# The last retained row's norm in three pieces, the output weights split by two engines, and the first output product one pair later

## The chip, the cores and the metric

One core of a Trainium2 chip runs the whole block. The metric is the device time of one execution in microseconds. TensorE multiplies, VectorE, ScalarE and GpSimd do the elementwise work, SyncE issues most of the transfers, and every engine works off its own queue in order and waits on semaphores for the others.

## What is computed

A streaming-encoder block of one layer on 1024 tokens of 1024 features, in f32. The input is normed and modulated (scale and shift from a conditioning vector), projected, and mixed by two groups of heads; group A is a sparse attention with 8 heads of 64, group B a retention with 8 heads of 64 and a norm of each head:

```python
    y = (inner + cross).reshape(B, S, H, d)
    mu = jnp.mean(y, axis=-1, keepdims=True)
    var = jnp.mean(jnp.square(y - mu), axis=-1, keepdims=True)
    y = (y - mu) * lax.rsqrt(var + EPS)
    return (jax.nn.silu(g.astype(jnp.float32)) * y).astype(dt).reshape(B, S, H * d)
...
    y = jnp.concatenate([y_a, y_b], axis=-1)
    return jnp.einsum('bse,ed->bsd', y, w_o)
```

The result is added to the input with a gate; after a second modulated norm a router sends each token to two of 32 small experts, and a last norm ends the block.

## The kernel before

Tokens lie on the 128 partitions, in 8 tiles (T = 8). Every large product is split: a number is written as a high part, rounded to the array's fast f32 format, and a low part, which is the rest, and `split_product` adds high times high, high times low and low times high, three matmuls of 512 columns for each 128 of depth. For each weight ScalarE therefore copies the high part and another engine subtracts it from the weight to get the low part.

**Start.** TensorE makes the row of modulation (L1770), ScalarE copies it out of PSUM (L833), and TensorE turns it into columns (L1777): groups g = 0, 1 are the two halves of the shift, g = 2, 3 those of the scale, each in PSUM bank g. One signal, `pe_cols`, stands behind all of them. VectorE adds the biases (L1126 to L1128) and then works in four parts of two k (blocks of 128 of depth): `hidden` modulates the normed input (L1134), ScalarE copies high parts (L849, L842), and `split_low` (L1183) and `hidden_low` (L1191) make the low ones. TensorE starts the input projection when the first low parts are there (L1748 to L1750).

**Retention.** For each tile t, `b_finish` on VectorE takes the values from PSUM (`b_yread`), then norms each head: mean, difference (L1409 to L1411), square and its mean (L1412 to L1414), gate (L1416), and a multiplication with the root that GpSimd makes (L712, L1418). SyncE stores the row (`store_retained`, L550). For the last tile the first step runs with the retention and all of the rest behind the first pair of heads of the attention, as one piece.

**Attention.** A list `order`, the same for all engines, sets the order of the work: tile after tile (i = 0 to 7) four pairs of heads (`heads`), then `rows`, with the products of earlier tiles between the pairs (`between`). A pair costs: logits on TensorE (L1898), `negated_logits` on VectorE (L1349), `exponent` on ScalarE (L954), turning of the weights on TensorE (L1974), their copy out of PSUM by ScalarE (L990), and the product with the values (L1987). TensorE issues the logits of the next pair ahead of the turning of this one. VectorE's logits run two heads ahead, so behind pair p it does those of pair p + 1. `rows` turns the sums' reciprocals (L1539, L2024) and the retained row (L2031) and makes high and low parts of the joined rows (L1544 to L1551; ScalarE L1003, L1006). `mix` is the output product of a tile in two halves of 512 columns, 24 matmuls each, with two VectorE operations (L1564, L1566) that scale it with the gate and add the input. `norm` and `turn` make the second norm (ScalarE L1012, GpSimd L725, VectorE L1573 to L1579) and turn it (L1755), `route` is the router's product.

The first `mix` needs the output weights in high and low parts, 8 blocks of 128x1024. They are loaded in two halves, blocks 4 to 7 (L584) and 0 to 3 (L588). ScalarE copies two blocks behind each of the four pairs of tile 0 (L998), in the order 4, 5, 6, 7, 0, 1, 2, 3. GpSimd subtracts for blocks 4 to 7 (L719), VectorE for blocks 0 to 3, behind the last pair of tile 0 and the first of tile 1 (L1532). SyncE's queue then has the store of the last retained row and a wait for it, ahead of all loads of the tiles: the retained row of tile 0 (L597), its input (L604), and four loads for the second norm and the router (L606 to L609). GpSimd waits for the last four and multiplies `sc2` with `g` (L721).

```python
        between[1] = [[], [("mix", (0, 0))], [("mix", (0, 1))], []]
```

## Time and profile before

| | us |
|---|---|
| three runs | 1575.22, 1575.89 (median), 1576.64 |
| profiled execution | 1575.17 |
| its span | 1573.0 |
| TensorE busy in it | 1420.4 (90%) |
| VectorE busy | 1098.9 (70%) |
| ScalarE busy | 906.5 (58%) |
| GpSimd busy | 272.8 (17%) |

The span runs from the first to the last instruction; the execution has some 2 us around it. Busy times say which engine is nearly full over the whole span, but a change in one place is worth what the waits of that place say. The granted clock is a share of TensorE's 2.4 GHz: 1.00 is 2.4 GHz and 0.50 is 1.2 GHz; its mean over the span is 0.955.

### The profile page before, as it was taken

How to read it: one execution, taken by the hardware profiler on the slowest of the kernel's cores; microseconds unless marked ns; L12 is line 12 of the kernel's file. 1: busy time of each engine (PE TensorE's matmuls, PEld its weight loads, DVE VectorE, ACT ScalarE, POOL GpSimd, SP SyncE). 2: the span in 40 equal slices, each digit the busy share in tenths (PEclk: the TensorE clock that was granted, in tenths of full speed). 3: DMA queues.
4: the chain of work that ended last, by engine and by line, in shares of the span. 5: the costliest groups of instructions: out<-in, count | busy, mean ns of one | idle time of the engine just before them, and what ended most of it. 6: DMA issues, size and time to landing. Idle time of an engine off the chain costs nothing.

```text
span 1573.0 us, 21452 instructions
## 1 busy us (share of the span) xinstructions
PE 1420.4 (90%) x7388; PEld 1109.4 (71%) x7388; DVE 1098.9 (70%) x1478; ACT 906.5 (58%) x1220; POOL 272.8 (17%) x192
## 2 busy tenths in 40 slices
PE   4899999999999897888899959999999999999980
PEld 2785447888888786556666747888888888888860
DVE  2726996642367984443344378999999999999968
ACT  5513767869974112434444425777777777777732
POOL 0000101320001012100000002232223322233115
PEclk9999999999999898789999979999999999999985
DMA  9213544555524234221111147999999999999986
GB/s 360 92 54 107 163 159 154 208 215 185 196 82 148 63 132 160 92 93 68 54 55 48 51 186 280 384 401 394 409 400 397 396 400 393 398 398 394 397 329 262
DMA packets 99076, 360.14 MB, mean 229 GB/s; under 512 B 11448, under 2 KB 23992, under 8 KB 74304
## 3 DMA queue, kind: packets, MB, share of 16 engines
q1 hardware_dynamic: 74816, 292.13, 49.0%
q0 software_dynamic: 11264, 33.57, 6.2%
q10 hardware_dynamic: 12928, 33.56, 5.4%
q8 instruction: 41, 0.67, 0.2%
q14 instruction: 27, 0.22, 0.0%
HBM read 306.76 MB, written 60.83 MB: 234 GB/s over the span
## 4 chain that ended last, share of the span: by engine, by line
PE 47%; DVE 5%; ACT 3%; issue 2%; DMA 1%; POOL 1%; ACTq 0%; DVEq 0%; POOLq 0%
PE PS L1748 13%; PE PS L1750 13%; PE PS L1749 13%; PE PS L2079 2%; PE PS L1898 1%; PE PS L1987 1%; PE PS L1974 1%; DMA WK<-xn_dram,gidx 1%; PE PS L2123 1%; DVE wlo L1510 1%; PE PS L2068 1%; ACT WK L954 1%; POOL BIG L777 1%; ACT WK L990 1%; DVE WK L1577 1%
## 5 line engine op out<-in xcount | busy, mean ns | idle before, releaser
L1510 DVE TENSOR_TENSOR wlo<-raw,whi 128x2048 fp32r<-128x2048 f32 x190 | 431.4, 2286 | 33.2 <-ACT whi L970 31.2
L970 ACT ACTIVATE whi<-raw 128x2048 fp32r<-128x2048 f32 x190 | 360.5, 1913 | 122.9 <-DVE WK L1673 80.8
L1748 PE MATMUL PS<-whi,xhi 128*128 128x512 f32 x512 | 203.7, 398 | 2.8 <-DVE xlo L1590 2.8
L1750 PE MATMUL PS<-whi,xlo 128*128 128x512 f32 x512 | 200.9, 392 | 0.0
L1749 PE MATMUL PS<-wlo,xhi 128*128 128x512 f32 x512 | 200.1, 391 | 0.0
L904 ACT ACTIVATE KV<-ACC,WK 128x1024 int8<-128x1024 f32 (+4 forms) x160 | 147.5, 925 | 24.7 <-DVE WK L1268 22.0
L744 POOL COPY wcol<-tw 128x1 f32 (+1 forms) x32 | 64.3, 2009 | 358.5 <-DVE WK L1696 358.5
L1748 PE MATMUL PS<-KVR,BIGR 128*128 128x512 f32 x304 | 120.4, 396 | 2.0 <-ACT WK L893 2.0
L1750 PE MATMUL PS<-KVR,BIGR 128*128 128x512 f32 x304 | 118.6, 390 | 0.0
L1749 PE MATMUL PS<-KVR,BIGR 128*128 128x512 f32 x304 | 118.3, 389 | 0.0
L1748 PEld LDWEIGHTS PS<-whi,xhi 128*128 128x128 f32 x512 | 96.9, 189 | 22.7 <-DVE xlo L1590 3.6
L1750 PEld LDWEIGHTS PS<-whi,xlo 128*128 128x128 f32 x512 | 96.5, 189 | 20.9
L1749 PEld LDWEIGHTS PS<-wlo,xhi 128*128 128x128 f32 x512 | 96.7, 189 | 19.2
L1748 PE MATMUL PS<-whi,hhi 128*128 128x512 f32 x256 | 104.3, 407 | 2.1 <-DVE hlo L1665 2.1
L1750 PE MATMUL PS<-whi,hlo 128*128 128x512 f32 x256 | 101.1, 395 | 0.0
L1749 PE MATMUL PS<-wlo,hhi 128*128 128x512 f32 x256 | 100.8, 394 | 0.0
L1245 DVE SCALAR_TENSOR_TENSOR ACC<-WK,wsc,ACC 128x384 f32<-128x384 f32 (+5 forms) x90 | 85.6, 952 | 9.8 <-ACT WK L893 6.9
L893 ACT ACTIVATE WK<-PS 128x384 f32<-128x384 f32 (+5 forms) x96 | 69.5, 757 | 36.6 <-PE PS L1875 28.7
L1875 PE MATMUL PS<-KV,BIG 64*128 64x512 f32 (+3 forms) x320 | 88.1, 555 | 1.0 <-DVE BIG L1165 0.9
L990 ACT ACTIVATE WK<-PS 128x512 f32<-128x512 f32 (+3 forms) x48 | 23.5, 539 | 100.6 <-PE PS L1974 100.5
L1875 PEld LDWEIGHTS PS<-KV,BIG 64*128 64x128 f32 x320 | 43.2, 190 | 49.6 <-issue 30.1
L862 ACT ACTIVATE WK<-PS 128x512 f32<-128x512 f32 x28 | 16.5, 595 | 106.2 <-PE PS L1750 62.4
(336 smaller groups left out, 2802.9 us busy)
## 6 DMA issues: line engine op xcount, KB each, us to landing
raw<-in_w_up SPq DMA_DIRECT2D x64, 1024.0 KB, 7.8
raw<-in_w_down SPq DMA_DIRECT2D x64, 1024.0 KB, 7.9
raw<-in_w_gate SPq DMA_DIRECT2D x62, 1024.0 KB, 8.1
WK<-in_w_ada POOLq DMA_DIRECT2D x16, 1024.0 KB, 5.9
y_dram<-zero ACTq DMA_DIRECT2D x8, 2048.0 KB
y_dram<-WK ACTq DMA_DIRECT2D x32, 512.0 KB
KV<-in_w_in SPq DMA_DIRECT2D x5, 2048.0 KB, 9.2
KV<-in_x SPq DMA_DIRECT2D x16, 512.0 KB, 5.2
```

The source lines that it names most:

```text
L744: nc.gpsimd.tensor_copy(wcol[:, s:s + 1], column).then_inc(G("m_w"), 1)
L893: own.go(A(WA["R"][:, u % 3, 0:K], PS[:, b:b + 2, :].rearrange("p b c -> p (b c)")[:, 0:K], ACT.Relu), G("sc_relu"))
L904: own.go(A(signs[i], ACC[:, ACC_OFF[i]:ACC_OFF[i] + K], ACT.Sign, bias=sel_try.bitcast(F32)[:, col:col + 1], accum_out=sel_count[:, col:co ...
L970: nc.scalar.activation(whi[:, slot], first_gate[q] if known(i, 1) and q in GATE else raw[:, q], ACT.Copy).then_inc(G("m_hi"), 1)
L990: own.go(A(PT[n % 4][:, 0:w], PS[:, 4 + n % 2, 0:w], ACT.Copy), G("c_pt"))
L1245: own(V.scalar_tensor_tensor(acc, R, wsc[:, i, h:h + 1], acc, ALU.mult, ALU.add), G("sc_acc"))
L1510: V.tensor_tensor(wlo[:, slot], first_gate[q] if known(i, 1) and q in GATE else raw[:, q], whi[:, slot].bitcast(F32), ALU.subtract)\
L1748: mm(out_, x_hi, w_hi, start=first, stop=False)
L1749: mm(out_, x_hi, w_lo, start=False, stop=False)
L1750: return mm(out_, x_lo, w_hi, start=False, stop=final)
L1875: last = mm(PS[:, 2 * (u % 3) + b, 0:w], qiT[rows, h // 2, tile(i)], kiD[rows, 512 * b:512 * b + w], start=True, stop=True)
L2079: last = tr(PS[:, k // 4, P * (k % 4):P * (k % 4) + P], spread[:, k], ident)
```

## The change

1. **Columns.** The columns are made in two halves (g = 0, 2, then 1, 3), in banks 0, 2, 6 and 7, with a signal behind each. VectorE takes the first half before its first part and the second before its third part.
2. **Norm of the last retained row.** `b_finish` has two more places to stop. For the last tile its pieces run behind the first, second and third pair of tile 0. Its result goes to a place of its own, so that nothing waits for its store; SyncE stores it at the second tile's turn, and waits for the store only before the last tile.
3. **Output weights.** GpSimd's subtractions go; VectorE makes all eight. ScalarE copies behind the pairs 1 to 5 (one, one, two, two, two blocks; pair 0 is the first), VectorE subtracts behind the pairs 2 to 6 in the same steps.
4. **Output product.** The two halves of tile 0's product run behind the third and the fourth pair of tile 1 instead of the second and the third. All output products take their blocks in the order 4 to 7, 0 to 3.

```diff
+COLUMN_BANKS = (0, 6, 2, 7)
+WO_HIGH = {1: (4,), 2: (5,), 3: (6, 7), 4: (0, 1), 5: (2, 3)}
+WO_LOW = {2: (4,), 3: (5,), 4: (6, 7), 5: (0, 1), 6: (2, 3)}
+        last_retained = KV[:, 7168:7680]
+        def retained(t):
+            return WB["y"] if t < T - 1 else last_retained
-        between[1] = [[], [("mix", (0, 0))], [("mix", (0, 1))], []]
+        between[1] = [[], [], [("mix", (0, 0))], [("mix", (0, 1))]]
...
-            store_retained(T - 1)
-            sp.wait_ge(G("st_yb"), 16 * T)
+            sp.wait_ge(G("st_yb"), 16 * (T - 1))
             for i in range(T):
+                if i == 1:
+                    store_retained(T - 1)
+                if i == T - 1:
+                    sp.wait_ge(G("st_yb"), 16 * T)
...
-            for k in range(4, KD):
-                pool.wait_ge(G("w_hi"), 4 * (ATTEND + 3) + WO_ORDER.index(k) + 1)
-                own.go(tt(wo_lo[:, k], wo[:, k], wo_hi[k].bitcast(F32), ALU.subtract), G("wo_lo"))
...
-                    quarter = 4 * i + lo // 2
-                    if quarter < 4:
-                        for k in WO_ORDER[2 * quarter:2 * quarter + 2]:
-                            act.wait_ge(G("ld_w0" if k >= 4 else "ld_w1"), 64)
-                            own.go(A(wo_hi[k], wo[:, k], ACT.Copy), G("w_hi"))
+                    for k in WO_HIGH.get(4 * i + lo // 2, ()):
+                        act.wait_ge(G("ld_w0" if k >= 4 else "ld_w1"), 64)
+                        own.go(A(wo_hi[k], wo[:, k], ACT.Copy), G("w_hi"))
...
+            def modulation(half):
+                ks = slice(4 * half, 4 * half + 4)
+                dve.wait_ge(G("pe_cols"), half + 1)
+                own.go(V.tensor_tensor(mod[:, 1, ks], PS[:, COLUMN_BANKS[half], 0:4], bc[:, 1, ks], ALU.add))
+                own(V.tensor_tensor(mod[:, 0, ks], PS[:, COLUMN_BANKS[2 + half], 0:4], bc[:, 0, ks], ALU.add))
+                own(V.scalar_tensor_tensor(mod[:, 0, ks], mod[:, 0, ks], 1.0, gc[:, ks], ALU.add, ALU.mult))
...
             for part in range(4):
                 ks = (2 * part, 2 * part + 1)
+                if part == 2:
+                    modulation(1)
...
                 own(V.tensor_tensor(y3, y3, small[:, 24:32].unsqueeze(2).to_broadcast(per), ALU.subtract))
+                yield
                 own(V.tensor_tensor(sq3, y3, y3, ALU.mult))
                 own(V.tensor_reduce(small[:, 24:32], sq3, X_AXIS, ALU.add))
                 own(V.tensor_scalar(small[:, 32:40], small[:, 24:32], 1.0 / HD, EPS, ALU.mult, ALU.add), G("norm_ms"))
+                yield
...
-                    if quarter == 0:
+                    if quarter < 3:
                         next(finish, None)
-                    if 3 <= quarter < 5:
-                        for k in (2 * quarter - 6, 2 * quarter - 5):
-                            dve.wait_ge(G("w_hi"), 4 * (ATTEND + 3) + WO_ORDER.index(k) + 1)
-                            own.go(V.tensor_tensor(wo_lo[:, k], wo[:, k], wo_hi[k].bitcast(F32), ALU.subtract),
-                                   G("w_lo"))
+                    for k in WO_LOW.get(quarter, ()):
+                        dve.wait_ge(G("w_hi"), 4 * (ATTEND + 3) + WO_ORDER.index(k) + 1)
+                        own.go(V.tensor_tensor(wo_lo[:, k], wo[:, k], wo_hi[k].bitcast(F32), ALU.subtract), G("w_lo"))
                 if kind == "rows":
-                    if i == 0:
-                        dve.wait_ge(G("st_yb"), 16 * T)
...
-            for g in range(4):
-                for b in range(4):
-                    rows = slice(32 * g, 32 * g + 32)
-                    last = mm(PS[:, g, b:b + 1], W0["row"][rows, P * b:P * b + P], ident[rows, 32 * g:32 * g + 1],
-                              start=True, stop=True)
-            last.then_inc(G("pe_cols"), 1)
+            for half in range(2):
+                for g in (half, 2 + half):
+                    for b in range(4):
+                        rows = slice(32 * g, 32 * g + 32)
+                        last = mm(PS[:, COLUMN_BANKS[g], b:b + 1], W0["row"][rows, P * b:P * b + P],
+                                  ident[rows, 32 * g:32 * g + 1], start=True, stop=True)
+                last.then_inc(G("pe_cols"), 1)
...
-                    for k in range(KD):
+                    for n, k in enumerate(WO_ORDER):
                         if i == 0 and h == 0:
-                            if k < 4:
-                                pe.wait_ge(G("w_lo"), 4 * (ATTEND + 3) + k + 1)
-                            else:
-                                pe.wait_ge(G("wo_lo"), k - 3)
+                            pe.wait_ge(G("w_lo"), 4 * (ATTEND + 3) + n + 1)
```

## Rows read from the trace of the kernel before

**Rows 1.** Windows of two stages: length, busy us of each engine (instructions), granted clock.

```profile
50.00:108.00 58.00, 58.00 (x269) 45.70 (x268) 29.33 (x66) 18.45 (x29) 1.68 (x2) 1.00 0.10 37
612.00:650.00 38.00, 23.91 (x131) 15.63 (x130) 20.99 (x46) 20.00 (x52) 14.21 (x6) 0.60 0.58 212
```

**Rows 2.** Timeline at the start: start us, us, engine, line, [idle before <-releaser].

```profile
40.46 2.47 PE L1777 MATMUL PS<-cst,WK 32*128 32x1 f32 x32 [0.78 <-ACT WK L833]
...
43.51 1.00 DVE L1134 TENSOR_SCALAR BIG<-BIG,mod 128x512 f32<-128x512 f32 x2
...
46.30 0.80 PE L1748 MATMUL PS<-ACCR,BIGR 128*128 128x512 f32 x1 [3.38 <-DVE BIGR L1191]
...
46.77 1.00 DVE L1134 TENSOR_SCALAR BIG<-BIG,mod 128x512 f32<-128x512 f32 x2
```

**Rows 3.** Timeline of tile 0 of the attention.

```profile
618.81 0.44 PE L1974 MATMUL PS<-cst,WK 128*128 128x128 f32 x2
...
620.02 2.00 ACT L998 ACTIVATE WOR<-BIG 128x1024 fp32r<-128x1024 f32 x2 [1.30 <-DMA BIG<-in_w_o]
...
620.94 0.17 DVE L1414 TENSOR_SCALAR small<-small 128x8 f32<-128x8 f32 x1
...
622.41 0.69 PE L1987 MATMUL PS<-KV,BIG 128*64 128x128 f32 x4 [3.16 <-ACT KV L990]
623.41 9.83 POOL L719 TENSOR_TENSOR BIGR<-BIG,WOR 128x1024 fp32r<-128x1024 f32 x4
623.43 2.86 DVE L1418 TENSOR_TENSOR WK<-WK,small 128x512 f32<-128x512 f32 x1 [1.60 <-POOL small L712]
...
626.89 0.80 PE L1898 MATMUL PS<-BIG,KV 64*128 64x128 f32 x4 [3.79 <-DVE nmax L1349]
```

**Rows 4.** Windows of four slices, for the granted clock (PEclk).

```profile
43.00:43.50 0.50, 0.00 (x0) 0.00 (x0) 0.41 (x3) 0.00 (x0) 0.00 (x0) 0.56 1.00 381
619.00:620.00 1.00, 0.25 (x2) 0.01 (x1) 0.97 (x2) 0.00 (x0) 0.00 (x0) 0.96 1.01 393
650.00:651.00 1.00, 1.00 (x5) 0.80 (x4) 0.00 (x0) 0.00 (x0) 0.00 (x0) 0.68 0.00 0
671.00:672.00 1.00, 0.48 (x8) 0.12 (x4) 1.00 (x1) 0.00 (x0) 0.00 (x0) 0.56 0.00 0
```

**Rows 5.** Chain of waits of 612 to 676: start us, us, what.

```profile
646.79 0.73 PE PS L1748
...
654.35 0.63 PE PS L1898 x4
...
656.76 0.43 PE PS L1748
...
662.59 0.70 DVE WK L1564
...
665.25 1.12 PE PS L2024 x16
```

**Rows 6.** Timeline of the rows of tile 0 and of tile 1.

```profile
635.62 1.97 PE L2024 MATMUL PS<-cst,ssum 128*64 128x128 f32 x16 [2.13 <-DVE ssum L1539]
...
639.98 2.21 DVE L1551 TENSOR_TENSOR WKR<-WK,WKR 128x512 fp32r<-128x512 f32 x1
...
642.93 1.23 PE L1898 MATMUL PS<-BIG,KV 64*128 64x256 f32 x4
```

**Rows 7.** Groups of 612 to 647 by form: busy us, mean ns | idle before.

```profile
L1532 DVE TENSOR_TENSOR BIGR<-BIG,BIGR 128x1024 fp32r<-128x1024 f32 x4 | 5.2, 1350 | 0.0
...
L954 ACT ACTIVATE WK<-WK,nmax 128x256 f32<-128x256 f32 x6 | 3.0, 502 | 0.9 <-DVE nmax L1349 0.9
...
L1349 DVE CUSTOM_DVE_ANT_0 WK<-PS,bias 128x256 f32<-128x256 f32 x6 | 2.4, 416 | 3.2 <-PE PS L1898 3.2
...
L990 ACT ACTIVATE KV<-PS 128x256 f32<-128x256 f32 x2 | 0.8, 384 | 1.2 <-PE PS L1974 1.2
```

**Rows 8.** DMA issues of 600 to 650: count, KB each, us to landing.

```profile
BIG<-in_w_o SPq DMA_DIRECT2D x2, 2048.0 KB, 9.4
```

More of the change, by code:

```diff
@@ L549, in store_retained @@
                 sp.wait_ge(G("b_out"), t + 1)
-                sp.dma_start(yb_dram[tile(t), :], WB["y"]).then_inc(G("st_yb"), 16)
+                sp.dma_start(yb_dram[tile(t), :], retained(t)).then_inc(G("st_yb"), 16)
             for step in range(3 * T):
@@ L1119, in _ @@
                        G("xn_ready"))
-            def halves(v):
-                return v.rearrange("p (h b) -> p h b", h=2)
+            def modulation(half):
[4 more added lines that the diff above has]
+                own(V.scalar_tensor_tensor(mod[:, 0, ks], mod[:, 0, ks], 1.0, gc[:, ks], ALU.add, ALU.mult))
             dve.wait_ge(G("hT_raw"), T)
-            dve.wait_ge(G("pe_cols"), 1)
-            own.go(V.tensor_tensor(halves(mod[:, 1, :]), PS[:, 0:2, 0:4], halves(bc[:, 1, :]), ALU.add))
-            own(V.tensor_tensor(halves(mod[:, 0, :]), PS[:, 2:4, 0:4], halves(bc[:, 0, :]), ALU.add))
-            own(V.scalar_tensor_tensor(mod[:, 0, :], mod[:, 0, :], 1.0, gc[:, :], ALU.add, ALU.mult))
+            modulation(0)
             def hidden(at, ks):
@@ L1417, in b_finish @@
                 dve.wait_ge(G("norm_rs"), t + 2)
-                own(V.tensor_tensor(y3, y3, small[:, 40:48].unsqueeze(2).to_broadcast(per), ALU.mult), G("b_out"))
+                own(V.tensor_tensor(retained(t).rearrange("p (h d) -> p h d", h=HB), y3,
+                                    small[:, 40:48].unsqueeze(2).to_broadcast(per), ALU.mult), G("b_out"))
             def late_rows():
@@ L1460, in _ @@
                     if t < T - 1:
-                        next(finish, None)
+                        for _ in finish:
+                            pass
                 narrow_some(2)
@@ L2040, in _ @@
                     part = slice(512 * h, 512 * h + 512)
-                    for k in range(KD):
+                    for n, k in enumerate(WO_ORDER):
                         if i == 0 and h == 0:
-                            if k < 4:
-                                pe.wait_ge(G("w_lo"), 4 * (ATTEND + 3) + k + 1)
-                            else:
-                                pe.wait_ge(G("wo_lo"), k - 3)
+                            pe.wait_ge(G("w_lo"), 4 * (ATTEND + 3) + n + 1)
                         last = split_product(PS[:, 7, :], yhi[:, k, :], ylo[:, k, :], wo_hi[k][:, part], wo_lo[:, k, part],
-                                             k == 0, k == KD - 1)
+                                             n == 0, n == KD - 1)
                     last.then_inc(G("b7_ready"), 1)
```

## The prediction

> **What bounds the kernel now.** I read the busy time by stage first [rows 1]. TensorE is the engine that is nearly full: 58.0 of 58.0 us from 50 to 108. VectorE and ScalarE are behind it. So time is lost where TensorE stands idle, and two such places touch the diff: the few us before the first input product, and the stretch from 612 to 650 (23.9 busy of 38 us, with a mean granted clock of 0.60).
>
> At the start, TensorE turns the modulation row into columns (32 instructions, 40.46 to 42.93); VectorE makes the modulation of them until 43.51; the first product of the input projection runs at 46.30 after 3.38 us of idle [rows 2]. After it TensorE is busy without a break until 108 [rows 1].
>
> In the second place, the timeline shows who is late. ScalarE's first two weight copies wait 1.30 us for the load of the output weights and then hold ScalarE to 622.02, so that the copy of the turned weights comes late and TensorE idles 3.16 us. VectorE works off the whole norm of the last retained row in one piece, waits 1.60 us for GpSimd's root, and its last multiplication takes 2.86 us, where an operation of its size (128x512, two operands in SBUF) should need well under 1: it stands beside GpSimd's four subtractions, which start 0.02 us before it. TensorE idles 3.79 us for the next logits [rows 3]. The clock falls to half (1.2 GHz) at the end of slice 619 to 620 and comes back in slice 650 to 651, after the first output product has started at 646.7 [rows 4, 5]. From there the chain of waits goes, with few gaps, through that product, a pair of heads, the second product, VectorE's two residual operations, and the rows of tile 1 at 665.25 [rows 5].
>
> **Part 1, columns in halves.** Before, VectorE waits for all 32 instructions (2.47 us) [rows 2]. After, it waits for the 16 of banks 0 and 2: 2.47/2 = 1.24 us less. Its three small operations (some 0.5 us, 43.0 to 43.51) are all fixed cost, as long on 4 columns as on 8. The second three, another 0.5 us, stand between VectorE's second and third part. Their cover: TensorE needs 24 products of 512 columns for the two k of one part, which is 24 x 0.235 = 5.6 us even at the full clock, while VectorE delivers a part each 3.25 us (43.51, 46.77) [rows 2]; by the third part it is over 4 us ahead. Cost 0. If the cover were gone it would be 0.5 us. The clock falls in slice 43.0 to 43.5 [rows 4], before the first product in both versions, and rises again during the products. If the rise keeps its distance from the first product the whole 1.24 us is won, if it stays at its time only half (the earlier work then runs at half clock): 0.6 to 1.24. I take **1.2**, because nothing says that the rise is tied to the kernel's start.
>
> **Part 2, tile 0 and 1 of the attention.** I write the schedule of the stretch anew with the durations of the rows, at half clock from 620 on: logits product 0.80 (tile 0) and 1.23 (tile 1), turning and values each 0.69 and, with twice the instructions, 1.1; VectorE's two passes over the logits 0.5 and 0.84; ScalarE's two copies 0.45 and 0.8, its two exponentials 0.8 and 1.0, one weight copy 1.0 to 1.05; VectorE's subtraction 1.2, from 5.2 for four, of which 0.5 is a delay by GpSimd [rows 3, 6, 7]. For tile 0 the short forms are estimates from those of tile 1, half as wide. The order on each engine is that of the code. The first pair, the turning of the second (to 619.25) [rows 3] and the norm's first three operations (to 619.5) are as before.
> Pair 2: logits to 620.0, norm piece 2 to 621.65; ScalarE copies to 619.75, exponentials 620.7, weight copy k=4 to 621.8 (its data lands at 620.02); values end 620.4.
> Pair 3: logits to 622.2; piece 3 waits for the root, which in the profile is used 2.3 us after the mean is ready (621.11 to 623.43) [rows 3], so 624.0 to 624.7; subtraction k=4 to 625.9; ScalarE copies 622.3, exponentials 623.1, k=5 to 624.2; values 623.1.
> Pair 4: logits 626.7, k=5 low 627.9; ScalarE copies 625.1, exponentials 627.5, k=6,7 to 629.5; values 625.8.
> Rows 0: the reciprocal at 627.9, and its product at 628.1 instead of 635.62. From there to the start of the last subtraction the profile has 4.4 us (639.98) [rows 6], so 632.5, end 633.2.
> Tile 1, pair 1: logits 634.1, k=6,7 low 636.5; copies 634.2, exponentials 635.2, k=0,1 high 637.3; values 635.4. Pair 2: logits 637.5, low k=0,1 639.9; copies 638.1, exponentials 639.1, k=2,3 high 641.2; values 639.3. Pair 3: logits 641.4, low k=2,3 643.8; copies 642.1; values 643.2.
> The first output product starts at 643.2 instead of 646.7 [rows 5]. It needs k=3 last, 21 of its 24 matmuls later, so the subtractions that end at 643.8 are hidden; without that cover they cost 0.6.
>
> What this holds of the parts: GpSimd's subtractions go (four in 9.83 us); VectorE gets four more, 4 x 1.2 = 4.8 us, but no longer stands some 2.2 us (2.86 less 0.7) in the norm and 0.5 in its own subtractions behind GpSimd [rows 3, 7]. ScalarE has the same eight copies, two fewer before the end of tile 0 (k=4 alone, then one, then two each). The store of the last retained row and its wait leave SyncE's queue ahead of the tile loads; what stood behind them (the retained rows, x, three rows of modulation, router weights: six loads) no longer waits for a multiplication that ends at 626.3, its store and the store's landing, so it issues at 616, right behind the output weights, instead of after 628.
>
> **GpSimd's one remaining big operation** (sc2 times g, 2.35 us) waits for those loads. The weights' two halves land 9.4 us after their issue on the mean [rows 8], the first after 7.5 (612.5 to 620.02) [rows 3], so the second after 11.3, at 626.8. These and the gate row, 4.7 MB, took 14.3 us from 612.5; the six loads behind them have 2.5 MB, so some 8 us more. So it starts near 635, beside VectorE's subtractions. The price of such a meeting in this kernel: 2.86 and 2.21 us for two multiplications and subtractions of some 0.7 [rows 3, 6], so 0 to 2.35 us on VectorE. Carried through the schedule, the full price moves the first product from 643.2 to 644.5, since ScalarE and TensorE have slack there. I take half, **643.8**. The Trainium skill (SBUF — State Buffer, "Who interferes with whom") says that VectorE with two SBUF inputs and a GpSimd instruction that reads SBUF exclude each other for a whole instruction and that the one issued first wins. The trace agrees: the 2.86 us are one of GpSimd's subtractions (9.83/4 = 2.5) and a little. By that rule the 2.35 us could still be paid once after the change, or nothing if VectorE is first.
>
> **Part 3, the product moved by one pair.** From 643.8: the product itself 7.56 us as before (646.72 to 654.28, its first part at half clock); the last pair of heads, 2.5 us as the pair between the products took (to 656.76); the second product 5.73 us (to 662.49) [rows 5]. It ends at 659.6. Before, the last pair stood after it and covered VectorE's work. Now VectorE must do two residual operations (0.70 each and a hand-over), then the reciprocal (0.2), while TensorE has nothing: 1.85 us with the hand-overs. Rows of tile 1 start at 661.4 instead of 665.25 [rows 5]. What follows (rows, norm, turn) has the same queue as before. Gain **3.8 us**; with 643.2 it is 4.4, with 644.5 it is 3.1. That products now take k in the order 4 to 7, 0 to 3 changes no count.
>
> **Sum.** 1.2 + 3.8 = 5.0 us. The profiled execution took 1575.17 us (span 1573.0 and 2.2 around it), the three runs 1575.22 to 1576.64, median 1575.89; it is 0.7 below the median. So 1570.2 for such an execution and 1570.9 for a median.
>
> **Rivals.**
> *A: the clock does not fall in tile 0.* For it: TensorE's two long gaps (3.16, 3.79) are gone; my longest gap there is 2 us. Against: the clock fell at 619.96, 0.7 us after TensorE's last work at 619.25, in a stretch that had gaps of no more than 1 us [rows 3, 4], and the change alters nothing before 619.5; in tile 1 it did not come back either, though the array had no long gap there: the logits product of 642.93 takes 1.23 us and that of 654.35 0.63 [rows 5, 6]. If it stayed up: product 7.56 to 5.73, rows of tile 0 0.9 us, the yb turning and the last values 0.4 us each shorter: 3.5 us more, 1567.4. The Trainium skill (TensorE: Matmul & The Clock Gate, "HAM oscillation — how this bites in real kernels") lays the half rate to idle gaps between bursts of matmuls; by it the removal of the long gaps would keep the clock. The row of 619 to 620 speaks against it here.
> *B: the new gap costs more.* After the second product TensorE idles 1.85 us and then has only rows and short products; before, the fall came at 671, in the middle of the norm [rows 4]. If it comes by the rows, they take 1.97 us as those of tile 0 did [rows 6] instead of 1.1 (half of it), 0.9 us more; with the full meeting with GpSimd (0.7) and half of the start's gain (0.6 lost) 2.8 us are left: 1573.1, hardly a difference.
> *C: no effect in tile 0 and 1.* VectorE's 4.9 us more fill the gap, another wait takes the old one's place, and the gap of 1.85 us stays. VectorE was busy 21.0 of 38 us in this stretch [rows 1], so there is room; only the start's 1.2 us would be won: 1574.7.
> *D, slower: the loads brought forward delay the output weights.* They now queue beside them. Against: the first 2 MB landed after 7.5 us though two more loads were behind them, the second after 11.3, as in a queue that is served in order [rows 3, 8]. If all nine shared the engines equally, the first half (1.0 MB of it and at most as much of each other load, 4.8 MB, at 0.33 to 0.42 MB a us from 616 on) would land near 629 instead of 620, ScalarE would stand 8 us at k=4 in pair 2, and with 5.0 us gained the result is 3 us slower: 1579. It decides from 5 us of delay on, a landing after 625.
>
> **How the numbers follow.** Forecast 0.62, A 0.11, B 0.14, C 0.07, D 0.06. A measurement of this kernel tells from no change about 0.2%, 3.2 us. Faster by more: forecast and A and a third of B, 0.77; within: most of B and C, 0.17; slower 0.06. The forecast's own range is the bounds of the start (0.6 to 1.24) and of GpSimd (3.1 to 4.4) and the 0.7 us by which runs differ: 1569.5 to 1572.9. For 8 in 10, A is taken in to its time and B to its: 1567.4 to 1573.6.
>
> **What would show it.** Right: first input product near 45.1; no four subtractions on GpSimd; the norm's last multiplication 0.69 us; first output product near 643 to 644, less the start's 1.2; rows of tile 1 near 661.4 less 1.2; a TensorE gap of some 1.9 us before them. Wrong: a ScalarE wait for the output weights beyond 1 us (D), a granted clock of 1.00 after 620 (A), VectorE operations of over 2 us in tile 1, or TensorE waiting for the last subtractions inside the first product.

## The result, and the profile after

The changed kernel takes 1568.21 us (median of 5 runs, 1562.82 to 1569.87) against 1575.89 before (median of 5, 1574.46 to 1576.64). The ratio is 0.9948 with a 95% interval of 0.9936 to 0.9961: 8.2 us faster, 6.1 to 10.1. Forecast were 1570.9 and 5.0 us. The way was right and the size too small: the time lies inside the prediction's range for 8 in 10 (1567.4 to 1573.6), but below the forecast's own (1569.5 to 1572.9), and 5.0 us lies below the interval of the gain. The profiled execution took 1569.87 us with a span of 1567.9, 5.1 less than before; it is the slowest of the five.

The timeline at the start:

```profile
40.96 2.47 PE L1787 MATMUL PS<-cst,WK 32*128 32x1 f32 x32 [0.78 <-ACT WK L841]
42.58 0.16 DVE L1130 TENSOR_TENSOR mod<-PS,bc 128x4 f32<-128x4 f32 x1 [17.56 <-PE PS L1787]
...
43.05 1.00 DVE L1141 TENSOR_SCALAR BIG<-BIG,mod 128x512 f32<-128x512 f32 x2
...
45.84 0.79 PE L1757 MATMUL PS<-ACCR,BIGR 128*128 128x512 f32 x1 [2.42 <-DVE BIGR L1198]
...
46.31 0.99 DVE L1141 TENSOR_SCALAR BIG<-BIG,mod 128x512 f32<-128x512 f32 x2
```
These rows answer to [rows 2]. The first column instruction comes 0.5 us later than before (the last load of modulation weights landed later in this execution), the first product 0.46 us earlier. The distance between them is 4.88 us instead of 5.84: 0.96 won, not 1.24. VectorE starts 1.62 us after the first column instruction, 0.38 behind the half of 2.47. The granted clock was back 4.7 us after the first product here and 3.6 us after it before; over all fourteen profiles it was 3.6 to 6.1 us, so the traces do not settle whether the rise moves with the start.

The timeline of tile 0 and the start of tile 1:

```profile
620.74 0.69 PE L1997 MATMUL PS<-KV,BIG 128*64 128x128 f32 x4 [0.37 <-ACT KV L998]
...
621.35 1.04 ACT L1004 ACTIVATE WOR<-BIG 128x1024 fp32r<-128x1024 f32 x1
...
621.36 0.80 PE L1908 MATMUL PS<-BIG,KV 64*128 64x128 f32 x4
621.96 0.17 DVE L1424 TENSOR_SCALAR small<-small 128x8 f32<-128x8 f32 x1
...
624.01 0.69 DVE L1429 TENSOR_TENSOR KV<-WK,small 128x512 f32<-128x512 f32 x1 [0.41 <-POOL small L723]
...
624.74 1.22 DVE L1544 TENSOR_TENSOR BIGR<-BIG,WOR 128x1024 fp32r<-128x1024 f32 x1
...
627.95 1.98 PE L2034 MATMUL PS<-cst,ssum 128*64 128x128 f32 x16 [1.28 <-DVE ssum L1548]
...
632.32 0.68 DVE L1560 TENSOR_TENSOR WKR<-WK,WKR 128x512 fp32r<-128x512 f32 x1
...
633.74 4.53 DVE L1544 TENSOR_TENSOR BIGR<-BIG,WOR 128x1024 fp32r<-128x1024 f32 x2
...
634.70 2.49 POOL L729 TENSOR_TENSOR BIG<-BIG 128x1024 f32<-128x1024 f32 x1 [10.79 <-DMA wr<-in_w_router]
```
This answers to [rows 3, 6]. ScalarE copies one block and waits for no load. TensorE waits 0.37 us ahead of the values of 620.74 and then goes straight on to the next logits (621.36), where it had idled 3.16 and 3.79. The last multiplication of the norm takes 0.69 instead of 2.86 us, the wait for the root ahead of it 0.41 instead of 1.60. The rows of tile 0 are at 627.95 instead of 635.62; the schedule in the prediction had 628.1. The one meeting with GpSimd that is left is plain to see: the two subtractions of 633.74 take 4.53 us, and GpSimd's multiplication (634.70, 2.49 us) stands beside them.

The granted clock, in windows (length, busy us of the engines, clock third from the end):

```profile
612.00:650.00 38.00, 30.34 (x171) 19.60 (x169) 25.31 (x56) 21.99 (x59) 4.12 (x2) 0.73 0.57 212
617.00:618.00 1.00, 0.96 (x6) 0.40 (x4) 0.41 (x3) 0.22 (x2) 0.00 (x0) 0.57 1.01 414
637.00:638.00 1.00, 0.53 (x4) 0.16 (x4) 1.00 (x1) 0.75 (x2) 0.19 (x1) 0.69 0.00 0
650.00:651.00 1.00, 0.47 (x8) 0.36 (x8) 0.97 (x4) 0.72 (x3) 0.00 (x0) 1.00 0.00 0
668.00:669.00 1.00, 1.00 (x5) 0.81 (x4) 0.00 (x0) 1.00 (x5) 0.00 (x0) 0.67 1.01 352
852.00:853.00 1.00, 0.38 (x2) 0.41 (x3) 0.97 (x2) 0.47 (x1) 0.00 (x0) 0.83 0.08 25
```
It answers to [rows 1, 4]. TensorE is busy for 30.3 of the 38 us instead of 23.9. The clock falls in the slice of 617, some 2.0 us after the first logits (before: 4.9), and comes back at 637.6, 5 us ahead of the first output product; before it came back 3.9 us into it. It falls again at 668.3 and, for some 3 us, at 852.7.

The timeline of the two output products of tile 0 (their first matmuls, and VectorE's operations behind them):

```profile
642.81 0.50 PE L1757 MATMUL PS<-WOR,WKR 128*128 128x512 f32 x1
...
648.82 0.69 DVE L1573 TENSOR_TENSOR WK<-PS,KV 128x512 f32<-128x512 f32 x1 [4.62 <-PE PS L1759]
...
651.23 0.50 PE L1757 MATMUL PS<-WOR,WKR 128*128 128x512 f32 x1
...
657.13 0.69 DVE L1573 TENSOR_TENSOR WK<-PS,KV 128x512 f32<-128x512 f32 x1 [5.82 <-PE PS L1759]
...
658.58 0.20 DVE L1548 RECIPROCAL ssum<-ssum 128x8 f32<-128x8 f32 x1
...
658.84 1.09 PE L2034 MATMUL PS<-cst,ssum 128*64 128x128 f32 x16 [1.75 <-DVE ssum L1548]
```
This answers to [rows 5]. The first product starts at 642.81, 27.7 us after the first logits of 615.12 (before 31.7 after 615.04), and reaches VectorE after 6.0 us instead of some 7.8. Behind the second one TensorE idles 1.75 us for VectorE's three operations; the prediction had 1.85. The rows of tile 1 start at 658.84 instead of 665.25.

Where the gain went: at the first norm the changed kernel is 6.4 us ahead (ScalarE's squares at 662.13 and 668.55), at that of tile 3 7.6, at that of tile 6 6.0, because of the fall at 852.7 which the execution before did not have, and 6.0 all through the experts. The last 1.0 us goes in the stage of the output.

### The profile page after: what moved, and what is told of

Its sections match the earlier page's. It is cut to its first block, busy times and chain, and to the rows that moved or that the text cites. A ratio compares the mean times of both kernels' runs of the same rounds, so it can differ in the third digit from the quotient of the medians.

```text
span 1567.9 us, 21456 instructions
## 1 busy us (share of the span) xinstructions
PE 1419.8 (91%) x7388; PEld 1108.7 (71%) x7388; DVE 1102.0 (70%) x1485; ACT 906.4 (58%) x1220; POOL 262.5 (17%) x188
## 4 chain that ended last, share of the span: by engine, by line
PE 47%; DVE 5%; ACT 3%; issue 2%; DMA 2%; POOL 1%; ACTq 0%; DVEq 0%; POOLq 0%
PE PS L1757 13%; PE PS L1759 13%; PE PS L1758 13%; PE PS L2086 2%; PE PS L1908 2%; PE PS L1997 1%; PE PS L1984 1%; DMA WK<-xn_dram,gidx 1%; PE PS L2130 1%; ACT WK L962 1%; DVE wlo L1523 1%; PE PS L2075 1%; POOL BIG L785 1%; ACT WK L998 1%; DVE WK L1586 1%
```

## The experiments

All runs are compared with the kernel before on the same chip. This table has what one profiled execution of each shows: the us from the first logits of the attention to (1) the start of the first output product, (2) the moment when the clock is back at 1.00, and (3) the rows of tile 1; (4) the us from the first product's start to the second's; again from the first logits, (5) the rows of tile 0 and (6) the moment when the clock falls; and the ratio of times to the kernel before with its interval. Moments of the clock are worked out from slices of 1 us.

| kernel | (1) product | (2) clock back | (3) rows of tile 1 | (4) first to second | (5) rows of tile 0 | (6) clock falls | ratio |
|---|---|---|---|---|---|---|---|
| before | 31.7 | 35.6 | 50.2 | 10.0 | 20.6 | 4.9 | |
| changed | 27.7 | 22.5 | 43.7 | 8.4 | 12.8 | 2.0 | 0.9948 (0.9936 to 0.9961) |
| columns_only | 32.0 | 35.8 | 50.5 | 9.9 | 21.0 | 1.7 | 0.9981 (0.9969 to 0.9992) |
| norm_only | 30.1 | 25.8 | 46.8 | 8.2 | 21.4 | 1.9 | 0.9991 (0.9975 to 1.0007) |
| weights_only | 25.6 | 19.1 | 42.6 | 8.4 | 15.9 | 2.1 | 0.9963 (0.9950 to 0.9975) |
| move_only | 36.3 | 39.5 | 53.8 | 9.9 | 20.8 | 1.9 | 1.0021 (1.0010 to 1.0031) |
| no_norm_pieces | 30.5 | 34.6 | 48.4 | 10.3 | 15.8 | 3.9 | 0.9972 (0.9961 to 0.9983) |
| no_columns | 27.0 | 31.4 | 45.0 | 10.4 | 12.3 | 4.0 | 0.9958 (0.9945 to 0.9972) |
| old_place | 23.3 | 28.2 | 42.3 | 10.4 | 12.3 | 4.3 | 0.9944 (0.9927 to 0.9960) |
| gpsimd_later | 27.1 | 31.8 | 45.2 | 10.5 | 12.3 | 4.4 | 0.9946 (0.9929 to 0.9963) |
| reciprocal_first | 27.7 | 22.5 | 42.9 | 8.4 | 12.8 | 2.0 | 0.9948 (0.9932 to 0.9964) |
| filled_gaps | 26.6 | 21.1 | 42.6 | 8.4 | 12.3 | 14.3 | 0.9948 (0.9932 to 0.9964) |
| old_place_later | 22.0 | 15.3 | 38.8 | 8.2 | 12.3 | 11.8 | 0.9939 (0.9920 to 0.9958) |
| all_three | 23.3 | 25.4 | 40.8 | 9.2 | 12.3 | 11.8 | 0.9935 (0.9922 to 0.9948) |

**Each part alone, on the kernel before.** The columns in halves (`columns_only`) have the diff of part 1 and nothing else.

> The kernel before with the columns in halves alone. Theory 1 (every part gives what its own queue arithmetic says): the distance from the first column instruction to the first input product falls from 5.84 to about 4.9 us, as in the changed kernel, and the time by 1 us (0 to 1.3, by where the clock rises). Theory 2 (the start gives nothing, since the clock's rise stays where it is): the distance falls, the time stays. The stretch from the first logits of the attention to the rows of tile 1 stays at 50.2 us in both.

The distance at the start is 4.88 us, the rows of tile 1 stay (50.5). The time falls by 3.0 us, with an interval of 1.3 to 4.9; 1 us (0 to 1.3) was expected. Theory 2 is out, and theory 1's size misses but for the edge. The profiled execution is the slowest of the twelve (1575.86), so its trace cannot show where 3 us come from.

The norm in pieces (`norm_only`; the edit also has the result's own place and the later store, as part 2 of the change):

```diff
                 own(V.tensor_tensor(y3, y3, small[:, 24:32].unsqueeze(2).to_broadcast(per), ALU.subtract))
+                yield
...
-                    if quarter == 0:
+                    if quarter < 3:
                         next(finish, None)
```

> The kernel before with the norm of the last retained row in three pieces, its own place and the later store alone; GpSimd still subtracts. Theory 1: ScalarE's wait for the weights still delays pair 2 and the last multiplication still meets GpSimd (over 2 us), so the rows of tile 1 come only 1 to 2 us earlier in their distance from the first logits (50.2 us before, 43.7 in the changed kernel). Rival: the norm in one piece was what held the attention; then most of the 6.5 us is won here, 4 us or more, and the time falls by as much.

```profile
625.57 11.15 POOL L727 TENSOR_TENSOR BIGR<-BIG,WOR 128x1024 fp32r<-128x1024 f32 x4
...
628.51 2.72 DVE L1428 TENSOR_TENSOR KV<-WK,small 128x512 f32<-128x512 f32 x1
...
631.95 5.86 DVE L1544 TENSOR_TENSOR BIGR<-BIG,BIGR 128x1024 fp32r<-128x1024 f32 x2
```
These are GpSimd's four subtractions and VectorE's work beside them (timeline). The rows of tile 1 come 3.4 us earlier, more than expected, but some 2 us of it are the clock, which is back before the product, and up to the rows of tile 0, where the clock is down in both, nothing is won: 21.4 us instead of 20.6. The norm still meets GpSimd: the last multiplication takes 2.72 us, and VectorE's own two subtractions 5.86 instead of 2.4. The time moves by 1.4 us within an interval that holds no change. The norm in one piece was not what alone held the attention.

The weights by ScalarE and VectorE alone (`weights_only`), with the product in its old place:

```diff
+WO_HIGH = {1: (4,), 2: (5,), 3: (6, 7), 4: (0, 1), 5: (2, 3)}
+WO_LOW = {2: (4,), 3: (5,), 4: (6, 7), 5: (0, 1, 2, 3)}
...
-            for k in range(4, KD):
-                pool.wait_ge(G("w_hi"), 4 * (ATTEND + 3) + WO_ORDER.index(k) + 1)
-                own.go(tt(wo_lo[:, k], wo[:, k], wo_hi[k].bitcast(F32), ALU.subtract), G("wo_lo"))
```

> The kernel before with the weights' split by ScalarE and VectorE over more pairs alone (GpSimd's four subtractions gone); norm in one piece with its store as before, product in its old place, columns whole. Theory 1 (the weights' part is the larger one): the last multiplication of the norm takes 0.7 instead of 2.9 us, the product starts 3 to 5 us closer to the first logits (31.7 before), rows of tile 1 at 45.5 to 47.5 instead of 50.2. Rival (norm and weights gain only together): 49 or more.

```profile
625.08 0.69 DVE L1415 TENSOR_TENSOR WK<-WK,small 128x512 f32<-128x512 f32 x1 [1.60 <-POOL small L714]
...
628.00 1.23 DVE L1528 TENSOR_TENSOR BIGR<-BIG,WOR 128x1024 fp32r<-128x1024 f32 x1
```
VectorE still stands 1.60 us for the root, but the multiplication takes 0.69 and its subtraction of one block 1.23 (timeline). The product starts 6 us earlier and the rows of tile 1 come 7.7 us earlier (42.6), of which some 2 are the clock; both are more than the 3 to 5 us and the 45.5 to 47.5 that were expected. Time 5.8 us less. This one part wins more in this stretch than the whole change. The edit holds two things, and no run parts them: GpSimd's subtractions go, and ScalarE's copies are spread over more pairs. Of the 4.7 us at the rows of tile 0, 2.0 are there at the logits of the fourth pair (9.8 us after the first logits instead of 11.9), as VectorE's multiplication is 2.2 us shorter; the other 2.6 come behind them, where ScalarE no longer makes two copies ahead of that of the turned weights and VectorE has one subtraction instead of two ahead of the reciprocals.

The move of the product by a pair (`move_only`):

```diff
-        between[1] = [[], [("mix", (0, 0))], [("mix", (0, 1))], []]
+        between[1] = [[], [], [("mix", (0, 0))], [("mix", (0, 1))]]
```

> The kernel before with the first output product one pair later and nothing else changed. Theory 1 (the move alone is a loss: it puts the third pair of tile 1, some 4 us, ahead of the product, and takes the last pair off VectorE's residual operations): the product starts 3 to 4 us later by its distance from the first logits (31.7 before), TensorE idles 1.8 us ahead of the rows of tile 1, and these come 1 to 3 us later than 50.2; time 1 to 3 us up, less or more by where the clock comes back. Rival: the pair fills an idle place, and the rows stay at 50.2.

```profile
669.60 0.69 DVE L1564 TENSOR_TENSOR WK<-PS,KV 128x512 f32<-128x512 f32 x1 [5.82 <-PE PS L1750]
...
671.31 0.88 PE L2024 MATMUL PS<-cst,ssum 128*64 128x128 f32 x12 [1.75 <-DVE ssum L1539]
```
The product starts 4.6 us later (3 to 4 were expected), the rows of tile 1 come 3.5 us later, the time rises by 3.3 us (1.6 to 4.9). TensorE idles 1.75 us behind the second product (timeline of VectorE and TensorE). The move is a loss by itself. At the start, where its code is that of the kernel before, this profile has 6.74 us from the first column instruction to the first product instead of 5.84:

```profile
41.33 3.37 PE L1777 MATMUL PS<-cst,WK 32*128 32x1 f32 x32 [0.78 <-ACT WK L833]
```
The columns take 3.37 us instead of 2.47; the granted clock is 0.83 in the slice of 42 and 0.50 in that of 43, so here it fell while they ran. The moment of the fall can thus be worth as much as part 1.

**One part taken out of the changed kernel.** With the norm in one piece again (`no_norm_pieces`, the diff of `norm_only` turned round):

> The changed kernel with the norm in one piece behind the first pair, as before, with its old place, store and wait; the weights' schedule, the product's place and the columns stay changed. Theory 1: VectorE stands 1.6 us for the root with the logits of two pairs behind it, the rows of tile 1 come 2 to 3 us later than in the changed kernel (distance from the first logits about 46), the time is 2 to 3 us over its 1568.2. Rival (the norm held it all): distance near 48 or more, time 4 us or more above. Rival (weights did it all): distance 43.7 to 44.5.

The rows of tile 1 are at 48.4, 4.7 us later; some 2 of them are the clock, which comes back 34.6 us after the first logits, and the product itself starts 2.8 us later. Time 0.9972, some 3.8 us above the changed kernel's. The distance is the one that the rival had for a norm that held it all (48 or more), but without the clock it is near theory 1's 46, and `norm_only` speaks against that rival. The rows of tile 0 are at 15.8 instead of 12.8. So the pieces win nothing while the weights are split in the old way (21.4 against 20.6), and 3 us once they are not.

Without the columns in halves (`no_columns`):

> The changed kernel without the columns in halves. Theory 1: the distance from the first column instruction to the first input product is 5.84 again instead of 4.88, and the time 0.5 to 1.3 us over the changed kernel. Theory 2 (the three us that the columns alone seemed to win are real): 2 us or more over it. In both the distance from the first logits to the rows of tile 1 stays near 43.7, but for the clock.

The distance at the start is 5.85. The ratio is 0.9958 instead of 0.9948, 1.6 us, between the two theories and with intervals that overlap. With `columns_only` the part is worth between 1.0 us (what the distance shows) and 3; more than the distance is not explained by anything that I see.

The product back in its old place (`old_place`):

```diff
-WO_LOW = {2: (4,), 3: (5,), 4: (6, 7), 5: (0, 1), 6: (2, 3)}
+WO_LOW = {2: (4,), 3: (5,), 4: (6, 7), 5: (0, 1, 2, 3)}
...
-        between[1] = [[], [], [("mix", (0, 0))], [("mix", (0, 1))]]
+        between[1] = [[], [("mix", (0, 0))], [("mix", (0, 1))], []]
```

> The changed kernel with the first output product back in its old place, behind the second pair of tile 1, and the last two subtractions one pair earlier to allow it. Theory 1: the move by a pair costs time, since it puts a pair of heads (3.9 us) ahead of the product and takes the last pair away that covered the two residual operations; the product starts near 639 and the rows of tile 1 come 2 to 3 us earlier than in the changed kernel (distance from the first logits about 41), time 1565 to 1566. Rival: the move is what gives the VectorE the room; then TensorE waits inside the product for the last low parts and the distance is 43.7 or more.

The product starts at 23.3 instead of 27.7. But the clock comes back 5 us into it, and the rows win only 1.4 us of the 4.4 at the start (2 to 3 were expected). Against a kernel of the same clock (`no_columns`, `gpsimd_later`, 45.0 and 45.2) they win 2.8. The time, 0.9944 (median 1567.34; 1565 to 1566 were expected), is no further down than the measurement can tell.

**What is left in the changed kernel.** GpSimd's multiplication put off (`gpsimd_later`):

```diff
             pool.wait_ge(G("ld_c"), 16 * 4)
+            pool.wait_ge(G("c_soft"), 18)
             own(tt(WC["sc2"], WC["sc2"], WC["g"], ALU.mult), G("pool_set"))
```

> The changed kernel; GpSimd's multiplication of sc2 with g also waits until VectorE has done its logits ahead of the second output product, so that it runs beside nothing. In the changed kernel the two subtractions of blocks 6 and 7 took 4.53 us instead of 2.4 beside it. Theory 1: they take 2.4 us, the last low part and the logits of pair 3 come 2 us earlier, the first output product starts 0.5 to 1.3 us closer to the first logits (27.7 in the changed kernel), and so do the rows of tile 1 (43.7). Rival: VectorE has slack there and the product does not move.

```profile
635.01 2.36 DVE L1545 TENSOR_TENSOR BIGR<-BIG,WOR 128x1024 fp32r<-128x1024 f32 x2
```
The same two subtractions take 2.36 us instead of 4.53 (timeline). The product starts at 27.05 instead of 27.69, but this is not shown to be the price of the meeting: 0.5 of the 0.6 us are there at the rows of tile 0 (12.3 instead of 12.8), long before GpSimd's multiplication, in a profile where the clock fell 2.4 us later. And `no_columns`, whose clock moved as here, has its product at 27.04 though GpSimd's multiplication (3.07 us) stands beside VectorE's next two subtractions:

```profile
636.20 3.01 DVE L1540 TENSOR_TENSOR BIGR<-BIG,BIGR 128x1024 fp32r<-128x1024 f32 x2
```
They lose 0.65 us there, and the product loses nothing. So the rival, that VectorE has slack there, is not out. The prediction had 1.3 us for the full meeting and took 0.6; no run shows either. The rows of tile 1 (45.2) are later than in the changed kernel, since the clock was down here until 31.8.

The reciprocals ahead of VectorE's wait (`reciprocal_first`):

```diff
-                    own(V.reciprocal(ssum[:, i % 2, :], ssum[:, i % 2, :]), G("c_over"))
+                    if i != 1:
+                        own(V.reciprocal(ssum[:, i % 2, :], ssum[:, i % 2, :]), G("c_over"))
...
                     i, h = i
+                    if (i, h) == (0, 1):
+                        dve.wait_ge(G("c_exp"), HA * 2)
+                        own(V.reciprocal(ssum[:, 1, :], ssum[:, 1, :]), G("c_over"))
```

> The changed kernel; VectorE makes the reciprocals of tile 1 ahead of its wait for the second output product, not behind the two residual operations. Theory 1 (the idle of TensorE behind the second product, 1.75 us in the changed kernel, is VectorE's residual pair and the reciprocal): the idle falls to 0.7 to 0.9 us, what VectorE's first residual operation needs, and the first norm comes 0.9 us earlier by its distance from the start of the second product. Rival: the rows wait for something else, and nothing moves.

```profile
658.69 0.69 DVE L1577 TENSOR_TENSOR WK<-PS,KV 128x512 f32<-128x512 f32 x1 [5.78 <-PE PS L1763]
...
659.53 1.09 PE L2038 MATMUL PS<-cst,ssum 128*64 128x128 f32 x16 [0.94 <-DVE WK L1577]
```
The idle falls from 1.75 to 0.94 us (timeline). The clock came back at the same 22.5 us as in the changed kernel, so the two compare directly: second product to first norm 10.12 instead of 10.90 us, 0.8 won of the 0.9 expected. It is too small for the times.

Extra matmuls in TensorE's gaps (`filled_gaps`; they add work and compute nothing that is used):

```diff
+                    if i < 2 and (i, lo) != (1, 6):
+                        for _ in range(2):
+                            mm(PS[:, 7, 0:256], kaT[:, 0, 0:P], kaT[:, 0, 0:256], start=True, stop=True)
                     values(i, lo, groups(i) - 1)
```

> The changed kernel with two extra matmuls of 128x256 f32 ahead of each pair's product with the values in tile 0 and in the first three pairs of tile 1, into a PSUM bank that nobody reads; it adds work to TensorE and changes nothing else. Theory 1 (the gaps of TensorE let the clock fall, and the clock's level is worth 1.8 us in the first product and 1 to 1.5 in the rows and values): the granted clock stays at 1.00 through most of the stretch, and the rows of tile 1 come up to 1.5 us earlier than 43.7. Rival: the clock falls all the same, and the extra matmuls at half clock (1.2 us a pair) delay the pairs by up to 4 us.

```profile
612.00:650.00 38.00, 32.56 (x201) 22.37 (x201) 24.43 (x60) 22.45 (x63) 4.45 (x2) 0.91 0.56 212
627.00:628.00 1.00, 0.26 (x3) 0.26 (x3) 0.86 (x2) 0.28 (x1) 0.00 (x0) 0.94 1.03 414
634.00:635.00 1.00, 1.00 (x7) 0.52 (x5) 0.00 (x0) 0.66 (x1) 1.00 (x1) 0.64 0.05 18
```
The clock (windows, third number from the end) falls at 627.9, 14.3 us after the first logits instead of 2.0, and is back at 634.7; its mean over 612 to 650 is 0.91 instead of 0.73. The rows come 1.1 us earlier than in the changed kernel. That would be what theory 1 says, but the same code of tile 0 without the extra matmuls kept the clock nearly as long in two other profiles, and over 612 to 650 its mean was higher in one of them than here. In `old_place_later` (windows):

```profile
626.00:627.00 1.00, 0.04 (x2) 0.04 (x2) 0.91 (x2) 1.00 (x3) 0.00 (x0) 0.74 1.06 406
629.00:630.00 1.00, 1.00 (x6) 0.67 (x6) 0.93 (x2) 0.00 (x0) 0.00 (x0) 0.55 1.00 401
612.00:650.00 38.00, 28.11 (x183) 20.06 (x182) 23.20 (x56) 21.44 (x58) 4.04 (x2) 0.96 0.57 212
```
There, and in `all_three`, the clock fell only 11.8 us after the first logits, in TensorE's wait of 2.8 us ahead of the rows of tile 0; in the other profiles of that code (column 6) it fell at 2.0 to 4.4. So one profile with filled gaps does not show that the gaps bring the clock down. The time is the same, 0.9948.

**Put together.** `old_place_later` has the old place and GpSimd's multiplication put off (`c_soft` at 16), `all_three` also the early reciprocals.

> The kernel with the product in its old place, and GpSimd's multiplication put off as well until VectorE's logits behind the first output product. Theory 1: product start at 23 us or a little less after the first logits, rows of tile 1 at 40.5 to 42.3, the lower value where the clock is back at the product's start; time 1 to 2 us under the changed kernel. Rival: the two together collide with VectorE's work for the product's last blocks, and nothing is won over the changed kernel.

> The changed kernel with the product in its old place, GpSimd's multiplication later, and the reciprocals of tile 1 ahead of VectorE's wait for the second product. Theory 1: as the kernel without the last edit, product start near 22 us after the first logits, rows of tile 1 at 38.8 with the clock up and some 2 more with it down, and up to 0.3 us less by the reciprocals, since a pair of heads covers most of that wait; time 1564 to 1566, the fastest of all. Rival: the earlier reciprocals hold VectorE's residual operations up, and it is no faster than the kernel without them.

In `old_place_later` the clock was down only from 11.8 to 15.3, before the product, and the rows are at 38.8, 11.4 us ahead of the kernel before and 4.9 ahead of the changed one. In `all_three` it came back 2 us into the product: 40.8. The ratios, 0.9939 and 0.9935, are the two lowest, 9.6 and 10.2 us under the kernel before; medians 1565.81 and 1567.15. They overlap with the changed kernel's interval, so the times alone do not show them faster than it. The traces show it for the stretch, in one execution each: `all_three` is 2.9 us ahead of the changed kernel there although its clock came back later. The early reciprocals of `all_three` were expected to give up to 0.3 us and the fastest time of all, 1564 to 1566; its median is over that of `old_place_later`, and the ratios cannot tell the two apart.

## Why the prediction was right, and where it was too small

The way and the path were forecast rightly. That the time stayed in the range for 8 in 10 is in part luck: at 1568.21 it lies nearer to rival A (1567.4) than to the forecast (1570.9), and the clock, which the prediction kept down until the first product, is what moved it there in the trace.

**The start** (1.2 us forecast) gives 0.96 in the distance. In the profile the rest of the way hides it: from the first product to the first logits of the attention the same code takes 568.0 to 571.8 us in the fourteen profiles. The cover for the second three operations held: TensorE never waits for VectorE there.

**Tile 0 and 1 at the schedule's count.** The rows of tile 0 came at 12.8 us after the first logits (forecast 13.1), the product at 27.7 (forecast 28.8, which is 643.8 less 615.04; 28.2 without GpSimd). The three stalls went as said, the loads stayed in order behind the weights (rival D is out: ScalarE waited for no load), and GpSimd's multiplication met VectorE's subtractions near 635 as worked out, at 2.2 us for VectorE; the 0.6 us that the sum took for the product is shown by no run. By the prediction's own list, VectorE's operations of over 2 us in tile 1 were a sign of being wrong, though its sum had this meeting in it at half its price. The schedule carried most of the forecast.

**The term that was mis-sized is the one for the product's length.** The prediction put it as "the product itself 7.56 us as before (646.72 to 654.28, its first part at half clock)". From the first product's start to the second's it gave 7.56 + 2.5 = 10.1 us; measured were 8.4, because the clock was back 5 us before the product. The start of the product was off by 1.1 us more, partly for the same reason: the last values before it took 0.66 us, not 1.1. From the second product to the rows the forecast held (7.5 us, measured 7.6). That makes the 2.6 us by which the rows of tile 1 (43.7 after the first logits) beat the forecast (46.4). In the kernels where the clock was down until the product (`no_columns` 45.0, `gpsimd_later` 45.2) the schedule was off by 1.3.

**Rival A was half right.** The clock did fall in tile 0, as the forecast said, even earlier. But it came back in tile 1, where the prediction argued from [rows 5, 6] that it would not. In the changed kernel TensorE ran without a break from the values of 634.05 to the turning that ends at 637.36, and the clock was back at 637.6. That is not the cause by itself: `no_columns` has the same run without a break, and its clock stayed at 0.50 for another 9.6 us (timeline, then windows):

```profile
632.82 1.12 PE L1992 MATMUL PS<-WK,BIG 128*64 128x128 f32 x8 [0.47 <-ACT WK L997]
633.87 1.23 PE L1903 MATMUL PS<-BIG,KV 64*128 64x256 f32 x4
635.02 1.11 PE L1979 MATMUL PS<-cst,WK 128*128 128x128 f32 x4
...
645.00:646.00 1.00, 1.00 (x4) 0.82 (x3) 0.00 (x0) 0.00 (x0) 0.00 (x0) 0.62 0.00 0
```
The prediction argued rival A with the rule of the Trainium skill (TensorE: Matmul & The Clock Gate, "HAM oscillation — how this bites in real kernels"), that idle gaps between bursts bring the half rate. The runs do not decide it: with filled gaps the fall comes at 14.3 us, but with the gaps of the changed kernel at anything from 2.0 to 11.8. Columns (2) and (4) of the table have the price: the clock back before the product, 8.2 to 8.4 us; well inside it, 9.9 to 10.5. That is 2 us which two kernels with the same schedule can differ by. Whether the clock came back early was not the same for kernels that hardly differ here (22.5 in the changed kernel, 31.4 in `no_columns`), so part of the 8.2 us measured may be how often it does; how often, the runs do not show, and what sets the moment stays open.

**Rival B** did not come: the clock held through the new gap until 668.3. **Rival C** is out.

**The move of the product (part 3 of the prediction) was counted rightly and judged too kindly.** The prediction worked out the new idle of 1.85 us (1.75) but never asked what the schedule would give without the move. The runs do: alone it costs 3.5 us in the stretch and 3.3 in time, and taken back in the changed kernel it gives 1.4 to 2.8. The change won in spite of it, by the weights' part and the pieces of the norm behind it.

What stays open: why the columns alone measured 3.0 us, and what of the 8.2 us of the whole, where the parts alone add up to 6.9 (3.0 + 1.4 + 5.8 - 3.3, each with its own interval), is clock and what is the parts helping each other.

## What to carry to other kernels

When two engines share work, ask which of them blocks the other before asking which is idle: GpSimd was 17% busy and looked free, but its subtractions stood in VectorE's way (2.86 us for a multiplication of 0.69). The part that took them off it, and spread ScalarE's copies, won more than all the rest. Two parts can hold each other: the norm in pieces won nothing alone and 3 us with the weights' part. Before a producer is given more time by moving its consumer later, look whether the consumer can start while its last inputs are still being made: here the product needed its last block 21 matmuls after its first, and the old place was free already. A schedule written out from rows holds to some 1 us over 30, but its matmul lengths hang on the clock's level: work out both levels and keep both for the range. And compare a reading of one profile with those of other kernels that have the same code there: here that took the ground from two explanations of the clock.

## What was not expected of the hardware

VectorE's subtractions beside GpSimd's are slowed by more than the one overlap: 5.86 us for two (2.36 alone) in `norm_only`, and GpSimd's four took 11.15 us there instead of 9.83 before, so both pay. GpSimd's root of 128x8 takes 1.64 us in the changed kernel and 2.08 in the kernel before, where VectorE multiplied two SBUF operands beside it. The Trainium skill (SBUF — State Buffer, "Who interferes with whom") has the lock for whole instructions; the rows of the operations of 128x512 and more agree with it. Those of GpSimd's small root do not quite: in the changed kernel VectorE's multiplication of 128x512 with both operands in SBUF started inside it and took 0.69 us all the same:

```profile
622.27 1.64 POOL L723 TENSOR_TENSOR small<-small,expo 128x8 f32<-128x8 f32 x1 [20.66 <-DVE small L1424]
...
622.92 0.69 DVE L1427 TENSOR_TENSOR WK<-WK 128x512 f32<-128x512 f32 x1
```

The time of the changed kernel spreads over 7 us in five runs (1562.8 to 1569.9); the mean granted clock of the fastest was 0.963 and of the slowest 0.958. The kernel before spread over 2.2 us in its five, but over 12.3 us (1571.31 to 1583.65) in the 17 runs beside `gpsimd_later`, so the spread is not the change's.
